# The sample sequences' depthwise convolution as products over windows and sums along the taps

## Chip, cores and metric

One core of a Trainium2 chip runs one launch of the kernel. The metric is the device time in microseconds of that launch, as the median of the runs; lower is better. The profiler's record of one execution gives the durations used below.

## The reference, cut to what matters

The reference runs one layer of a decoder trunk for two groups of tokens that share all weights: a prompt of 1024 tokens, and 8 sample sequences of 8 tokens each. A layer is an FFN, a mixer of two branches (a Conformer convolution and an mLSTM with 4 heads), and a second FFN. The change touches the causal depthwise convolution alone, of width 31 over 1024 channels:

```python
def _causal_dwconv(u, buf, w, b):
    full = jnp.concatenate([buf.astype(u.dtype), u], axis=1)
    y = lax.conv_general_dilated(full, w[:, None, :].astype(u.dtype), window_strides=(1,), padding='VALID',
                                 dimension_numbers=('NWC', 'WIO', 'NWC'), feature_group_count=u.shape[-1])
    return y + b, full[:, -(CONV_WIDTH - 1):]
```

For the prompt `buf` is zero; for each sample sequence it holds the last 30 inputs of its past. Every output is a sum of 31 products, one per tap, plus a bias per channel.

## The kernel before

Everything lies with the features on the 128 partitions and the tokens in the free dimension: 1024 prompt columns and then 64 sample columns (8 sequences of 8), 1088 in all, padded to 1092 so that they split into three PSUM banks of 364. The 1024 features are 8 tiles of 128. All arithmetic is float32.

**The products.** The weights come in units of 128 x 1024. SP loads each (L333), POOL splits it into a high part (L543) and a low part (L545), and PE makes three passes over it (L575: high by high, high by low, low by high). There are two buffers of split weights, so POOL may split a unit only when PE is done with the unit two before it. These two POOL instructions come once per unit, and both read SBUF.

**The mixer** goes head by head (`H` is 4). The first three heads are one loop on each engine, the last is written out. Each head has two sections.

In section A, PE runs 8 units (q, k, v and o of this head), ACT evicts them, and DVE does `taps(h)` (L1365): the depthwise convolution of two feature tiles of this head. Its input lies in `glu` (2 tiles of 30 zeros and 1024 prompt columns) and `glus` (2 tiles, 8 sequences, 30 columns of past and 8 of their own). `taps` copies the two tiles' weights to `dw_cur` (L1370, L1372) and then goes over the 31 taps (L1373). At each tap it drains DVE (L1376) and issues four instructions: for each of the two tiles one over the 1024 prompt columns and one over the 64 sample columns. Tap 0 is a `tensor_scalar` with the bias (L1388), the other 30 are a `scalar_tensor_tensor` (L1390; the profile shows them at the helper's line, L1072) that adds the product of one shifted slice by one weight to the output in `y`. Before tap 15 `prelude(h)` (L1350) prepares the head's gate columns and signals `head_ready`.

In section B, PE runs 8 units (4 in the last head) and threads the pieces of the mLSTM in between, each a chain over PE, ACT and DVE with small tiles (`ktok`, `vaug`, `vws`, `dw`, `tin`, `hn_p`, `hn_s`, `hs_p`, `hs_s`). Its first DVE instruction is the copy to `ap_h` (L1465), which stands behind `taps` in DVE's order. The first piece's transposes to `bank_x` (PE, L748) wait for it. SP waits for `taps_done` (L433) before it loads the next head's past into `glus`.

The order of the work on each engine is the order of the code. Semaphores order the engines against each other, and `drain` orders DVE against itself.

Of the kernel before, what the change touches and what calls it, by code (L numbers as in the profile page):

```python
# [24 lines left out]

ACT = mybir.ActivationFunctionType
F32 = mybir.dt.float32
F32R = mybir.dt.float32r
I32 = mybir.dt.int32

P = 128
D = 1024
KT = D // P
NP = 1024
NB, TB = 8, 8
NT = NP + NB * TB
# [8 lines left out]
CW = 31  # L45
# [5 lines left out]
C1 = HD + 1  # L51
# [76 lines left out]
def trunk(nc, t_in, t_out):  # L128
    with ExitStack() as ctx:

        at = [(nc.sbuf_base + 63) // 64 * 64]

        def region(nbytes):
            start = at[0]
            at[0] += (nbytes + 31) // 32 * 32
            assert at[0] <= nc.sbuf_usable_end, (at[0], nc.sbuf_usable_end)
            return start

        def place(name, shape, dt, offset):
            return nc.alloc_sbuf_tensor_at(name, shape, dt, offset=offset)  # L140

        def own(name, shape, dt=F32):
            return place(name, shape, dt, region(int(np.prod(shape[1:])) * 4))
# [7 lines left out]
        r_x = region(KT * TILE)  # L151
        x = place("x", [P, KT, W], F32, r_x)
        qkvo = place("qkvo", [P, 8, W], F32, r_x)
        a_hi = place("a_hi", [P, KT, W], F32R, r_x)
        a_tmp = place("a_tmp", [P, KT, W], F32, r_x)
        r_y = region(KT * TILE)
        y = place("y", [P, KT, W], F32, r_y)
        a_lo = place("a_lo", [P, KT, W], F32R, r_y)
        work = place("work", [P, KT, W], F32, r_y)
        sg, prod, ss, rstd = (work[:, i] for i in (0, 1, 2, 3))  # L160
# [7 lines left out]
        glu = own("glu", [P, 2, PAST + NP])  # L168
        glus = own("glus", [P, 2, NB, PAST + TB])
        st = own("st", [P, 3, 2, C1])  # L170
        c_cur = own("c_cur", [P, 2, C1])
        ktok = own("ktok", [P, HD])
        vaug = own("vaug", [P, C1])
        vws = own("vws", [P, C1])
        dw = own("dw", [P, P])
        tin = own("tin", [P, C1])
        hn_of = {kind: own(f"hn_{kind}", [P, C1]) for kind in "ps"}
        hs_of = {kind: own(f"hs_{kind}", [P, HD]) for kind in "ps"}
        g_row = own("g_row", [4, NT])
        g_cur = own("g_cur", [4, NT])  # L180
        if at[0] < r_z + KT * TILE:
# [10 lines left out]
        dw_cur = place("dw_cur", [P, 2, CW], F32, r_tmp)  # L192
        b_ada = own("b_ada", [P, NMOD * KT])
        b_in = own("b_in", [P, H, 16])
        vecs = own("vecs", [P, 8, KT])
# [26 lines left out]
        NORM1, NORM2, NORM3, NORMF, B_DW, LN_G, LN_B, MH = range(8)  # L222
# [55 lines left out]
        def bank3(s):  # L278

            return slots[:, s, :, 0:GW]  # L280

        def tile3(ap):
            return ap.rearrange("p (g n) -> p g n", g=3)
# [5 lines left out]
        def sample3(ap64):  # L289
            return ap64.rearrange("p (b t) -> p b t", b=NB)  # L290
# [33 lines left out]
        def _(sp):  # L324
# [75 lines left out]
            def head(h, n_units):  # L400
# [8 lines left out]
                for n in range(n_units):  # L409
# [10 lines left out]
                    if n_units == 4 and n == 3:  # L420
                        for k in range(2, 6):
                            sp.dma_start(qkvo[:, k - 2, :], b_keep[k // 2, :, k % 2, :]).then_inc(b_back[k], 16)
                    load_unit()
                    s, _, freed = jobs.take_unit()
                    t = n // 2 if n_units == 8 and n < 4 else n % 2
                    if n_units == 4 and n == 0:
# [36 lines left out]
            for t in range(2):  # L463
                load_unit()
                load_unit()
                jobs.take_unit()
                s, _, freed = jobs.take_unit()
                sp.wait_ge(slot_free[s], freed)
                sp.wait_ge(glus_in, 32)
                conv_stores(0, t)  # L470
# [370 lines left out]
        def _(act):  # L841
# [6 lines left out]
            def squares(p):  # L848

                for k in range(KT):  # L850
# [6 lines left out]
                    if sqs.n >= 2:  # L857
                        act.wait_ge(sq_added, sqs(-1))
                    act.activation(sq[k % 2][:, 0:NT], x[:, k, 0:NT], ACT.Square).then_inc(sq_done, 1)
                    sqs.add()  # L860

            def root(dst):

                s, done, _ = jobs.take_part()
                act.wait_ge(part_done, done)
                act.activation(tile3(dst), bank3(s), ACT.Sqrt, bias=eps[:, 0:1]).then_inc(slot_free[s], 1)

            def norm(p):
# [3 lines left out]
                for k in range(KT):  # L872
                    act.wait_ge(t_ready, p * KT + k + 1)
                    act.activation(u_hi[:, k, 0:NP], tn[k % 2][:, 0:NP], ACT.Identity, bias=sh[:, k, 0:1])
                    act.activation(u_hi[:, k, NP:NT], tn[k % 2][:, NP:NT], ACT.Copy).then_inc(hi_ready, 1)

            def ffn():
                def gate():
                    s, done, _ = jobs.take_unit()
                    act.wait_ge(unit_done, done)  # L880
                    act.activation(tile3(sg), bank3(s), ACT.Silu).then_inc(slot_free[s], 1)

                def high(j, up):
                    act.wait_ge(slot_free[up[0]], up[2])
                    act.activation(hid_hi[:, j, :], prod, ACT.Copy).then_inc(hid_hi_done, 1)  # L885

# [179 lines left out]
        def _(dve):  # L1066
# [4 lines left out]
            def stt(out, in0, scalar, in1, op0, op1):  # L1071
                return dve.scalar_tensor_tensor(out=out, in0=in0, scalar=scalar, in1=in1, op0=op0, op1=op1)  # L1072
# [259 lines left out]
            for n in range(4):  # L1332
# [4 lines left out]
                src = bank[0:L].rearrange("p (c q e) -> p c q e", c=4, q=4)[:, :, :, 0:4]  # L1337
# [12 lines left out]
            def prelude(h):  # L1350

                of_head = (lambda t, n: t[:, :, h:16:4]) if isinstance(h, int) else (
                    lambda t, n: t.rearrange("p c (q h) -> p c q h", q=4)[:, :, :, bass.ds(h, 1)].rearrange("p c q h -> p c (q h)"))
                sel = ident[0:4, h:h + 1] if isinstance(h, int) else ident[0:4, bass.ds(h, 1)]
                dve.drain()
                dve.wait_ge(c_out, 16 * heads(1))
                dve.wait_ge(b_out, 16 * heads(1))
                dve.tensor_copy(col_h[:], of_head(col[:], NC))
                dve.tensor_copy(cols_h[:], of_head(cols[:], NB))
                dve.tensor_scalar(g_cur[:], g_row[:], sel, -1.0, ALU.mult, ALU.mult)  # L1360
                dve.tensor_scalar(apm[:], apv[:], sel, None, ALU.mult)
                dve.memset(c_cur[:], 0.0).then_inc(head_ready, 1)
                heads.add()

            def taps(h):  # L1365

                tiles = [2 * h, 2 * h + 1]
                pick = lambda t: (y[:, tiles[t], :] if isinstance(h, int) else y[:, bass.ds(tiles[t], 1), :].rearrange("p a n -> p (a n)"))
                if isinstance(h, int):
                    dve.tensor_copy(dw_cur[:], w_dw[:, 2 * h:2 * h + 2, :])  # L1370
                else:
                    dve.tensor_copy(dw_cur[:], w_dw[:, bass.ds(2 * h, 2), :])  # L1372
                for j in range(CW):  # L1373
                    if j == CW // 2:
                        prelude(h)
                    dve.drain()  # L1376
                    if j == 0:
                        dve.wait_ge(glus_in, 32 * heads(1))
                        for t in range(2):
                            dve.wait_ge(conv_out[t], 16 * convs[t]())  # L1380
                    for t in range(2):
                        yt = pick(t)
                        w = dw_cur[:, t, j:j + 1]
                        for out, src in ((yt[:, 0:NP], glu[:, t, j:j + NP]),
                                         (sample3(yt[:, NP:NT]), glus[:, t, :, j:j + TB])):
                            if j == 0:
                                b = vecs[:, B_DW, 2 * h + t:2 * h + t + 1] if isinstance(h, int) else vecs[:, B_DW, bass.ds(2 * h + t, 1)]
                                last = dve.tensor_scalar(out, src, w, b, ALU.mult, ALU.add)  # L1388
                            else:
                                last = stt(out, src, w, out, ALU.mult, ALU.add)  # L1390
                last.then_inc(taps_done, 1)

            def section_a(h):
                taps(h)
                for _ in range(8):
                    jobs.take_unit()
# [96 lines left out]
            for k in range(1, KT):  # L1493
                last = dve.tensor_tensor(ysum, y[:, 0, :] if k == 1 else ysum, y[:, k, :], ALU.add)
# [173 lines left out]
```

## Time and profile before

| quantity | value |
|---|---|
| median of 3 runs | 3418.11 us |
| lowest and highest run | 3416.35 and 3418.35 us |
| span of the profiled execution | 3417.0 us |
| PE busy | 3167.0 us (93%) |
| DVE busy | 1597.9 us (47%) |
| POOL busy | 1020.0 us (30%) |
| ACT busy | 465.6 us (14%) |

The page gives the profiled execution's span, from its first to its last instruction; it gives no separate time for that execution, so the 1.1 us between span and median is taken as what lies around the span. The busy share of an engine is an average over stages with different limits. What section A is worth is read from its own stretch, and from who waits for whom at its end.

### The profile page before, as it was taken

How to read it: one execution, taken by the hardware profiler on the slowest of the kernel's cores; microseconds unless marked ns; L12 is line 12 of the kernel's file. 1: busy time of each engine (PE TensorE's matmuls, PEld its weight loads, DVE VectorE, ACT ScalarE, POOL GpSimd, SP SyncE). 2: the span in 40 equal slices, each digit the busy share in tenths (PEclk: the TensorE clock that was granted, in tenths of full speed). 3: DMA queues.
4: the chain of work that ended last, by engine and by line, in shares of the span. 5: the costliest groups of instructions: out<-in, count | busy, mean ns of one | idle time of the engine just before them, and what ended most of it. 6: DMA issues, size and time to landing. Idle time of an engine off the chain costs nothing.

```text
span 3417.0 us, 47244 instructions
## 1 busy us (share of the span) xinstructions
PE 3167.0 (93%) x18860; PEld 3029.7 (89%) x18860; DVE 1597.9 (47%) x2811; ACT 465.6 (14%) x746; POOL 1020.0 (30%) x449
## 2 busy tenths in 40 slices
PE   8999999999968889879888997989998999999995
PEld 8999999999958778878787895789887999999995
DVE  5122233222276943973694397476344233232335
ACT  2000000000031122012112211322012000000001
POOL 1233333333312311321231142034332333333331
PEclk9999999999989999999999998999998999999997
DMA  6312121212121112212211221222210111111111
GB/s 221 106 62 74 61 74 61 74 61 68 49 75 41 44 42 68 70 34 60 74 50 42 68 70 51 60 103 93 108 50 25 44 44 44 47 43 43 43 43 59
DMA packets 83136, 217.63 MB, mean 64 GB/s; under 512 B 28352, under 2 KB 28480, under 8 KB 82496
## 3 DMA queue, kind: packets, MB, share of 16 engines
q1 hardware_dynamic: 83000, 215.86, 19.7%
q8 instruction: 88, 1.44, 0.2%
q14 instruction: 40, 0.33, 0.0%
q10 hardware_dynamic: 8, 0.00, 0.0%
HBM read 184.03 MB, written 31.81 MB: 63 GB/s over the span
## 4 chain that ended last, share of the span: by engine, by line
PE 73%; DVE 16%; issue 5%; DVEq 3%; POOL 1%; DMA 1%; ACT 1%; SPq 0%; ACTq 0%; POOLq 0%
PE slots L575 61%; DVE y L1072 12%; PE bank_x L637 3%; PE bank_x L758 2%; DVEq L1376 2%; PE bank_x L750 1%; PE bank_x L765 1%; PE bank_y L762 1%; PE bank_y L767 1%; DVE work L1100 1%; PE bank_y L637 1%; DMA w_raw<-w_units_dram 1%; PE bank_y L740 1%; PE bank_x L775 0%; PE bank_x L748 0%
## 5 line engine op out<-in xcount | busy, mean ns | idle before, releaser
L543 POOL TENSOR_TENSOR w_hi<-w_raw,one 128x1024 fp32r<-128x1024 f32 x220 | 437.9, 1990 | 2317.9 <-PE slots L575 2247.3
L575 PE MATMUL slots<-u_hi,w_hi 128*128 128x364 f32 (+1 forms) x4032 | 930.3, 339 | 53.0 <-DVE u_lo L1133 20.2
L575 PE MATMUL slots<-u_hi,w_lo 128*128 128x364 f32 (+1 forms) x4032 | 899.5, 332 | 0.0
L575 PE MATMUL slots<-u_lo,w_hi 128*128 128x364 f32 (+1 forms) x4032 | 898.4, 331 | 0.0
L575 PEld LDWEIGHTS slots<-u_hi,w_hi 128*128 128x128 f32 x4032 | 699.4, 191 | 81.4 <-issue 65.4
L575 PEld LDWEIGHTS slots<-u_hi,w_lo 128*128 128x128 f32 x4032 | 705.3, 190 | 9.2 <-issue 8.7
L575 PEld LDWEIGHTS slots<-u_lo,w_hi 128*128 128x128 f32 x4032 | 708.2, 191 | 0.0
L545 POOL TENSOR_TENSOR w_lo<-w_raw,w_hi 128x1024 fp32r<-128x1024 f32 x220 | 581.3, 2642 | 17.2
L1163 DVE TENSOR_TENSOR work<-work,slots 128x1092 f32<-128x1092 f32 x44 | 56.9, 1292 | 913.5 <-PE slots L575 913.5
L1072 DVE SCALAR_TENSOR_TENSOR y<-glu,dw_cur,y 128x1024 f32 (+1 forms) x240 | 344.7, 1436 | 9.1
L1072 DVE SCALAR_TENSOR_TENSOR x<-slots,m_g,x 128x728 f32<-128x728 f32 x368 | 257.8, 742 | 0.0
L575 PE MATMUL slots<-hid_hi,w_hi 128*128 128x364 f32 (+1 forms) x1056 | 237.4, 333 | 11.1 <-DVE hid_lo L1168 9.6
L575 PE MATMUL slots<-hid_lo,w_hi 128*128 128x364 f32 (+1 forms) x1056 | 233.8, 330 | 0.0
L575 PE MATMUL slots<-hid_hi,w_lo 128*128 128x364 f32 (+1 forms) x1056 | 232.3, 328 | 0.0
L575 PEld LDWEIGHTS slots<-hid_hi,w_hi 128*128 128x128 f32 x1056 | 183.6, 190 | 12.1 <-DVE hid_lo L1168 10.0
L885 ACT ACTIVATE hid_hi<-work 128x1092 fp32r<-128x1092 f32 x44 | 49.2, 1118 | 1030.5 <-PE slots L575 733.7
L575 PEld LDWEIGHTS slots<-hid_lo,w_hi 128*128 128x128 f32 x1056 | 183.5, 189 | 0.0
L575 PEld LDWEIGHTS slots<-hid_hi,w_lo 128*128 128x128 f32 x1056 | 183.3, 189 | 0.0
L1146 DVE TENSOR_TENSOR xs_tmp<-slots,m_g 128x64 f32<-128x64 f32 x184 | 41.4, 225 | 289.1 <-PE slots L575 288.1
L1072 DVE SCALAR_TENSOR_TENSOR y<-glus,dw_cur,y 128x64 f32 (+1 forms) x240 | 149.3, 622 | 0.0
L637 PEld LDWEIGHTS bank_x<-cs,ada 128*128 128x128 f32 x896 | 119.4, 212 | 5.3 <-issue 5.3
L637 PE MATMUL bank_x<-cs,ada 128*128 128x9 f32 x896 | 116.2, 267 | 5.3 <-DMA ada<-ada_units_dram 5.3
(219 smaller groups left out, 2187.4 us busy)
## 6 DMA issues: line engine op xcount, KB each, us to landing
w_raw<-w_units_dram SPq DMA_DIRECT2D x220, 512.0 KB, 3.6
ada<-ada_units_dram SPq DMA_DIRECT2D x72, 512.0 KB, 4.2
st<-state_dram SPq DMA_DIRECT2D x32, 257.0 KB, 3.7
C_s_out<-st SPq DMA_DIRECT2D x32, 257.0 KB, 3.6
x_keep<-x SPq DMA_DIRECT2D x1, 4368.0 KB, 12.7
ga_keep<-th SPq DMA_DIRECT2D x8, 546.0 KB, 5.6
gb_keep<-th SPq DMA_DIRECT2D x8, 546.0 KB, 5.6
th<-gb_keep SPq DMA_DIRECT2D x8, 546.0 KB, 4.6
```

The costliest lines, as they stand in the source:

```text
L543: pool.tensor_tensor(w_hi[:, slot, :], w_raw[:, slot, :], one[:].to_broadcast([P, D]), ALU.mult).then_inc(w_hi_done, 1)
L545: pool.tensor_tensor(w_lo[:, slot, :], w_raw[:, slot, :], w_hi[:, slot, :].bitcast(F32), ALU.subtract).then_inc(w_split, 1)
L575: last = pe.matmul(slots[:, s, g, 0:b - a], w_of(w), r[:, k, a:b], start=(k == 0 and q == 0), stop=(k == K - 1 and q == 2))
L637: last = pe.matmul(b[:, 16 * j:16 * j + NV], ada[:, j, k * P:(k + 1) * P], cs[:, k, :], start=(k == 0), stop=(k == KT - 1))
L740: pe.matmul(bank_y[0:L, 0:L], k_of(m, a, L), q_of(m, a, L), start=(m == 0), stop=(m == 1))
L750: last = pe.matmul(bank_x[0:L, n * P:(n + 1) * P], src, ident[:], start=True, stop=True)
L758: last = pe.matmul(bank_x[0:L, 0:C1], q_of(m, a, L), mem[:, m, :], start=(m == 0), stop=(m == 1))
L885: act.activation(hid_hi[:, j, :], prod, ACT.Copy).then_inc(hid_hi_done, 1)
L1072: return dve.scalar_tensor_tensor(out=out, in0=in0, scalar=scalar, in1=in1, op0=op0, op1=op1)
L1146: dve.tensor_tensor(sample3(xs_tmp[:]), sample3(slots[:, s, 2, LP:LP + NB * TB]), per_batch(g[:, 1:NV]), ALU.mult)
L1163: dve.tensor_tensor(tile3(prod), tile3(sg), bank3(s), ALU.mult).then_inc(slot_free[s], 1)
L1376: dve.drain()
```

## The change

The prompt's 31 steps stay, two instructions a tap instead of four. The sample columns leave the loop. After tap 0 and ahead of tap 1 a new function `conv_of_sample` runs. For each of the two tiles and each half of the 8 sequences it makes one `tensor_tensor` product and one `tensor_reduce`:

- the product reads `glus` through an access pattern of overlapping windows (4 sequences, 8 positions, 31 taps), multiplies it by the tile's 31 weights, repeated over sequences and positions, and writes 992 columns to the new tile `win`;
- the sum goes along the 31 taps and writes 32 columns of `y`.

A drain stands before each of these eight instructions, and another before the two `tensor_scalar` that add the bias to 64 columns each.

`win` has no memory of its own: it lies over `ktok`, `vws`, `dw`, `tin` and part of `hn_p`, which section B uses and section A does not. `vaug`, whose last column of ones must stay, is moved ahead of it.

```diff
@@ -24,6 +24,7 @@
 from concourse.alu_op_type import AluOpType as ALU
 
 ACT = mybir.ActivationFunctionType
+AX = mybir.AxisListType
 F32 = mybir.dt.float32
 F32R = mybir.dt.float32r
 I32 = mybir.dt.int32
@@ -169,13 +170,16 @@
         glus = own("glus", [P, 2, NB, PAST + TB])
         st = own("st", [P, 3, 2, C1])
         c_cur = own("c_cur", [P, 2, C1])
+        vaug = own("vaug", [P, C1])
+        r_win = at[0]
         ktok = own("ktok", [P, HD])
-        vaug = own("vaug", [P, C1])
         vws = own("vws", [P, C1])
         dw = own("dw", [P, P])
         tin = own("tin", [P, C1])
         hn_of = {kind: own(f"hn_{kind}", [P, C1]) for kind in "ps"}
         hs_of = {kind: own(f"hs_{kind}", [P, HD]) for kind in "ps"}
+        win = place("win", [P, NB // 2 * TB, CW], F32, r_win)
+        assert at[0] >= r_win + NB // 2 * TB * CW * 4
         g_row = own("g_row", [4, NT])
         g_cur = own("g_cur", [4, NT])
         if at[0] < r_z + KT * TILE:
@@ -1362,6 +1366,25 @@
                 dve.memset(c_cur[:], 0.0).then_inc(head_ready, 1)
                 heads.add()
 
+            def windows(t, b):
+
+                first = glus[:, t, b:b + NB // 2, 0:TB]
+                return bass.AP(first.tensor, first.offset, [*first.ap, [1, CW]])
+
+            def conv_of_sample(pick, bias):
+
+                for t in range(2):
+                    for b in (0, NB // 2):
+                        dve.drain()
+                        dve.tensor_tensor(win[:].rearrange("p (b t) j -> p b t j", b=NB // 2), windows(t, b),
+                                          dw_cur[:, t, :].unsqueeze(1).unsqueeze(1).to_broadcast([P, NB // 2, TB, CW]), ALU.mult)
+                        dve.drain()
+                        dve.tensor_reduce(pick(t)[:, NP + b * TB:NP + (b + NB // 2) * TB], win[:], AX.X, ALU.add)
+                dve.drain()
+                for t in range(2):
+                    out = pick(t)[:, NP:NT]
+                    dve.tensor_scalar(out, out, bias(t), None, ALU.add)
+
             def taps(h):
 
                 tiles = [2 * h, 2 * h + 1]
@@ -1370,7 +1393,10 @@
                     dve.tensor_copy(dw_cur[:], w_dw[:, 2 * h:2 * h + 2, :])
                 else:
                     dve.tensor_copy(dw_cur[:], w_dw[:, bass.ds(2 * h, 2), :])
+                bias = lambda t: (vecs[:, B_DW, 2 * h + t:2 * h + t + 1] if isinstance(h, int) else vecs[:, B_DW, bass.ds(2 * h + t, 1)])
                 for j in range(CW):
+                    if j == 1:
+                        conv_of_sample(pick, bias)
                     if j == CW // 2:
                         prelude(h)
                     dve.drain()
@@ -1379,15 +1405,12 @@
                         for t in range(2):
                             dve.wait_ge(conv_out[t], 16 * convs[t]())
                     for t in range(2):
-                        yt = pick(t)
+                        out, src = pick(t)[:, 0:NP], glu[:, t, j:j + NP]
                         w = dw_cur[:, t, j:j + 1]
-                        for out, src in ((yt[:, 0:NP], glu[:, t, j:j + NP]),
-                                         (sample3(yt[:, NP:NT]), glus[:, t, :, j:j + TB])):
-                            if j == 0:
-                                b = vecs[:, B_DW, 2 * h + t:2 * h + t + 1] if isinstance(h, int) else vecs[:, B_DW, bass.ds(2 * h + t, 1)]
-                                last = dve.tensor_scalar(out, src, w, b, ALU.mult, ALU.add)
-                            else:
-                                last = stt(out, src, w, out, ALU.mult, ALU.add)
+                        if j == 0:
+                            dve.tensor_scalar(out, src, w, bias(t), ALU.mult, ALU.add)
+                        else:
+                            last = stt(out, src, w, out, ALU.mult, ALU.add)
                 last.then_inc(taps_done, 1)
 
             def section_a(h):
```

## Rows read from the trace of the kernel before

**Rows 1.** The page: its first line, and part 4, the chain that ended last, by line.

```profile
span 3417.0 us, 47244 instructions
...
PE slots L575 61%; DVE y L1072 12%; PE bank_x L637 3%; PE bank_x L758 2%; DVEq L1376 2%; PE bank_x L750 1%; PE bank_x L765 1%; PE bank_y L762 1%; PE bank_y L767 1%; DVE work L1100 1%; PE bank_y L637 1%; DMA w_raw<-w_units_dram 1%; PE bank_y L740 1%; PE bank_x L775 0%; PE bank_x L748 0%
```

**Rows 2.** Waits of PE, whole run and second head; columns: us in total, times, longest.

```profile
PE bank_x L748 <- DVE ap_h L1465: 80.9, 4, 25.5
...
PE bank_x L748 <- DVE ap_h L1465: 17.4, 1, 17.4
```

**Rows 3.** Busy time of each engine in one stretch, the second head's taps.

```profile
core 0: us, PE busy (x) PEld busy (x) DVE busy (x) ACT busy (x) POOL busy (x), PEclk, DMA share, GB/s
1380.73:1504.30 123.57, 106.30 (x630) 105.61 (x628) 120.23 (x131) 12.00 (x11) 42.40 (x16) 0.93 0.13 42
```

**Rows 4.** Line 1072 writing y, all heads (ns min/median/max); last row from page part 5.

```profile
L1072 DVE SCALAR_TENSOR_TENSOR y<-glu,dw_cur,y x240: 1272/1283/3412, 1084.2 to 2096.0; 128x1024 f32 x90, 128x1024 f32<-128x1024 f32 x30
L1072 DVE SCALAR_TENSOR_TENSOR y<-glus,dw_cur,y x240: 271/278/2427, 1085.4 to 2097.2; 128x64 f32 x90, 128x64 f32<-128x64 f32 x30
...
L1072 DVE SCALAR_TENSOR_TENSOR y<-glus,dw_cur,y 128x64 f32 (+1 forms) x240 | 149.3, 622 | 0.0
```

**Rows 5.** Timeline of DVE, start of the second head's taps; columns: start us, us.

```profile
1381.42 0.81 DVE L1388 TENSOR_SCALAR y<-glu,dw_cur,vecs 128x1024 f32 x1 [0.49 <-issue]
1382.15 0.31 DVE L1388 TENSOR_SCALAR y<-glus,dw_cur,vecs 128x64 f32 x1
...
1383.49 1.28 DVE L1072 SCALAR_TENSOR_TENSOR y<-glu,dw_cur,y 128x1024 f32 x1
1384.69 0.28 DVE L1072 SCALAR_TENSOR_TENSOR y<-glus,dw_cur,y 128x64 f32 x1
1384.89 1.28 DVE L1072 SCALAR_TENSOR_TENSOR y<-glu,dw_cur,y 128x1024 f32 x1
1386.08 0.28 DVE L1072 SCALAR_TENSOR_TENSOR y<-glus,dw_cur,y 128x64 f32 x1
1386.44 1.28 DVE L1072 SCALAR_TENSOR_TENSOR y<-glu,dw_cur,y 128x1024 f32 x1
```

**Rows 6.** Timeline of DVE and of POOL around one split of weights, second head.

```profile
1394.92 1.92 DVE L1072 SCALAR_TENSOR_TENSOR y<-glus,dw_cur,y 128x64 f32 x1
1396.91 3.40 DVE L1072 SCALAR_TENSOR_TENSOR y<-glu,dw_cur,y 128x1024 f32 x1
...
1394.17 2.59 POOL L543 TENSOR_TENSOR w_hi<-w_raw,one 128x1024 fp32r<-128x1024 f32 x1 [22.69 <-PE slots L575]
1396.84 2.40 POOL L545 TENSOR_TENSOR w_lo<-w_raw,w_hi 128x1024 fp32r<-128x1024 f32 x1
```

**Rows 7.** Nearest DVE instructions: timeline of a drained series, then lines 1100, 1098, 1279.

```profile
2254.69 8.15 DVE L1494 TENSOR_TENSOR a_tmp<-a_tmp,y 128x1092 f32<-128x1092 f32 x6
...
L1100 DVE TENSOR_TENSOR work<-work x28: 1291/1292/3460, 33.9 to 3388.0; 128x1088 f32<-128x1088 f32 x28
...
L1098 DVE COPY work<-work x4: 727/728/2266, 33.1 to 3367.0; 128x1088 f32<-128x1088 f32 x4
...
L1279 DVE TENSOR_TENSOR_SCAN g_row<-rows,mc x8: 471/472/2652, 1035.2 to 1044.3; 4x128 f32<-4x128 f32 x8
L1279 DVE TENSOR_TENSOR_SCAN g_row<-rows,ms x8: 208/208/224, 1045.0 to 1046.0; 4x8 f32<-4x8 f32 x8
```

**Rows 8.** Timeline in the first FFN: a DVE product that reads PSUM, and POOL.

```profile
567.88 1.29 DVE L1163 TENSOR_TENSOR work<-work,slots 128x1092 f32<-128x1092 f32 x1 [21.71 <-PE slots L575]
...
567.99 1.90 POOL L543 TENSOR_TENSOR w_hi<-w_raw,one 128x1024 fp32r<-128x1024 f32 x1 [9.41 <-PE slots L575]
```

**Rows 9.** Timeline of DVE and of POOL, start of the first head's taps.

```profile
1082.12 0.81 DVE L1388 TENSOR_SCALAR y<-glu,dw_cur,vecs 128x1024 f32 x1 [4.76 <-DMA conv_s_out<-glus]
...
1086.58 2.03 POOL L543 TENSOR_TENSOR w_hi<-w_raw,one 128x1024 fp32r<-128x1024 f32 x1 [11.50 <-PE slots L575]
1088.68 2.39 POOL L545 TENSOR_TENSOR w_lo<-w_raw,w_hi 128x1024 fp32r<-128x1024 f32 x1
```

## The prediction

> **What bounds the kernel now.** I read the page first. The span is 3417.0 us, and the chain that ended last is PE's for 61%, but 12% of it is DVE's line 1072 writing `y`, and 2% more is DVE's queue at L1376, the drain of the tap loop [rows 1]. So the taps are on the path for part of the run. The waits of PE say where: its longest wait is for the copy to `ap_h`, the first DVE instruction behind the taps, four times and 80.9 us in all; in the second head it is 17.4 us [rows 2]. The busy times of the second head's taps agree: in 123.57 us DVE is busy for 120.23, PE for 106.30 [rows 3]. In section A, DVE is the bound of every head, and PE idles for over 17 us at its end. So what `taps` gains or loses, up to 17.4 us a head, goes one to one into the span. What it gains would be lost again only behind PE's own end, which lies far beyond the effects below.
>
> **Why the listed busy time misleads.** The 64-column steps show a median of 278 ns and a maximum of 2427; the 1024-column ones 1283 and 3412 [rows 4]. The page's mean of 622 ns for a 64-column step [rows 4] would make 60 x 0.62 = 37 us a head. I go by start to start instead. In an undisturbed tap the starts are 1383.49, 1384.69, 1384.89, 1386.08 and 1386.44 [rows 5]: the first sample step takes 0.20 us of the time, the second 0.36 (with the drain). A whole tap is 2.95 us.
>
> The long ones come from POOL. When it splits a unit, a sample step takes 1.92 us and the next prompt step 3.40; they end within 0.1 us of the ends of POOL's two instructions, 1396.76 and 1399.24 plus the step itself [rows 6]. DVE loses (1.92 - 0.28) + (3.40 - 1.28) = 3.76 us per split, whichever instruction is hit. POOL has 16 instructions in this stretch [rows 3], so eight splits, one per unit. The account closes: 0.69 (copy and issue) + 2.07 (tap 0) + 30 x 2.95 + 8 x 3.76 = 121.3, which leaves 2.2 us of the 123.6 for the prelude. A removed sample step that stood in a split does not take the stall with it: the next prompt step stands there instead. The splits' times are PE's, and all eight still fall within the taps.
>
> **Removed, per head.** The 30 pairs of `scalar_tensor_tensor`. The next prompt step then starts 1.20 us behind the first, as a step behind a step does now, and the second one is followed by the drain at once. A drained series of DVE instructions shows what that costs: 6 products of 1.30 us take 8.15, so (8.15 - 1.30) / 5 = 1.37 from start to start, a gap of 0.07 [rows 7]. A tap becomes 1.20 + 1.28 + 0.07 = 2.55 us, which saves 0.40; 30 taps save **12.0**. Tap 0 goes from 1383.49 - 1381.42 = 2.07 [rows 5] to 0.73 + 0.81 + 0.07 = 1.61, which saves **0.46**.
>
> **Added, per head.** Four products of 992 columns with both inputs in SBUF. The nearest row is the product of 1088 columns, 1.291 us undisturbed [rows 7]; less 96 columns at (1283 - 278) / 960 = 1.05 ns [rows 4] it is 1.19. Four sums of 992 columns: the trace has no reduction along columns. From below the bound is the copy, 0.728 us for 1088 columns [rows 7], so 0.65. From above it is the scan, the one instruction here that carries a sum: (472 - 208) / 120 = 2.2 ns a column [rows 7], which makes 992 columns 2.37 us. I take 1.19, as for a product, to which it is nearer than to the scan: it reads each column once and hands on one sum per 31. With a gap of 0.07 after each, 4 x (1.19 + 1.19 + 0.14) = **10.1**. The two bias adds of 64 columns are 2 x 0.31 [rows 5] + 0.07 = **0.7**. Together 10.8.
>
> The Trainium skill (VectorE: DVE Perf Modes, the perf-mode tier table) has `tensor_reduce` at one element a cycle in every case; by its 0.96 GHz and the (N + 151) / 0.96 that it gives for a product, an estimate for the sum is 1.19 us, and the total would be as forecast.
>
> **Net** 12.46 - 10.8 = 1.7 us a head, 6.7 us in four.
>
> **The first head gains more.** Its taps start at 1082.12, so the new block runs from 1083.73, and POOL wants the port at 1086.58 [rows 9]. A DVE product of which one input is in PSUM is not held up by POOL: it takes its usual 1.29 us although POOL starts 0.11 us later, and POOL takes its usual 1.90 [rows 8]. A sum also has one SBUF input and runs at one column a cycle in my forecast, so I let it run beside POOL. Walking through: the second product ends at 1087.4 and POOL's first instruction runs to 1089.3 beside the second sum; the third product waits 0.6 us; POOL's second runs to 1092.9 beside the third sum; the fourth product waits 1.1. That is 1.6 lost in place of 3.8, a gain of **2.1**. In the second head (the others are alike) the block begins at 1381.42 + 1.61 = 1383.0, its last sum ends at 1393.1, and POOL begins at 1394.17 [rows 6]: nothing there.
>
> The Trainium skill (SBUF — State Buffer, Who interferes with whom) says the same: two SBUF inputs contend with a reading POOL, and `tensor_reduce` never does. [rows 6] and [rows 8] agree for products.
>
> **Edits at nothing.** Where `win` and `vaug` lie costs no instruction. The signal to SP moves with the end of the taps; its load of `glus` is needed a whole section later. The extra drains find DVE empty. Register work for the new dynamic addresses hides behind the instructions running; uncovered it would be a few tenths a head.
>
> **Sum.** 6.7 + 2.1 = 8.8 us off the profiled span: 3408.2, and with the 1.1 us around it **3409.3 us** (-0.26%). A measurement here can tell about 0.2%, 6.8 us, from no change, so the edge of faster lies at 3411.3, where the sum would take 1.32 us instead of 1.19.
>
> **Rivals.**
>
> 1. *Small prices eat it; no change to be seen.* Sixteen products and sixteen sums stand in the path, so 0.13 us more on one kind costs 2 us. If POOL holds up the sums as well, the first head's gain goes: 3411.4. One mechanism would be the windows themselves: runs of 31 words that start on odd words half the time. Against it, prompt steps start on odd columns at every other tap, and their minimum and median are 1272 and 1283 ns [rows 4]; for it, no row has short odd runs. At one lost column per run, 32 x 1.04 ns x 16 = 0.5 us: 3409.8. With the first head's gain gone and the sums at 1.5 us it is 3416. Chance of this case 0.32.
>  The Trainium skill (Vector Engine (DVE) Microarchitecture Reference, Measured stream behaviour on trn2) gives 1.30 ns a column in place of 1.05 for word pairs starting on an odd word; if the products took that, the total would be 3413.2 by an estimate from its figures. The prompt steps' rows speak against it for long runs; none here shows short ones.
>
> 2. *The sum goes at the scan's rate; slower.* Place: the four `tensor_reduce` of each head, each drained before and after, with nothing beside them on the path. At 2.37 us each, 16 x 1.18 = 18.9 us more than forecast: 3428.2. It decides from 1.19 + 8.8 / 16 = 1.74 us a sum on (no gain left), and shows as slower from 2.17 on. For it: the scan also carries a running value from column to column. Against it: the scans work on only four partitions and are another instruction; nothing else on DVE at full size is that slow but the reciprocal. Chance 0.09.
>
> 3. *The stalls go with the sample steps.* If the time that the sample steps spend blocked went with them, a head would save 37 - 10.8 = 26 us, PE would become the bound, and the 80.9 us of its waits would go: 3337. [rows 6] speaks against it: the prompt step is blocked as well as the sample step. Chance 0.02.
>
> **How the numbers follow.** The forecast case has 0.57, rival 1 0.32, rival 2 0.09, rival 3 0.02. Faster is the forecast with rival 3, less a little for its upper edge, 0.57; same is rival 1 with that little, 0.34; slower 0.09. The range leaves out rivals 2 and 3 and the copy-rate end of the sum (16 x 0.54 = 8.6 us further down, 3400.7), and takes in most of what lies between: 3403 to 3417.
>
> **What would show it.** In the changed profile: prompt steps in a tap at starts 1.20 and 1.35 apart; 16 products and 16 sums near 1.19 us; PE's four waits for `ap_h` down by 1.7 us each, by 3.8 in the first head; POOL's first split of the first head beside a sum; section B of unchanged length. A sum of over 1.3 us, a tap that stays above 2.7 us, or dynamic addresses that leave gaps of issue between the new instructions would prove the forecast wrong.

## The result, and the profile after

| | kernel before | changed kernel |
|---|---|---|
| median of 20 runs | 3418.73 us | 3410.73 us |
| lowest and highest | 3416.35 and 3423.96 us | 3405.28 and 3419.52 us |
| profiled execution, span | 3417.0 us | 3411.4 us |
| DVE busy | 1597.9 us | 1582.5 us |
| PE's waits for `ap_h` | 80.9 us | 71.6 us |

The ratio is 0.9973, with a 95% interval of 0.9967 to 0.9980: 8.0 us less by the medians, where 8.8 less (3409.3 us) was forecast. The changed kernel's runs scatter more widely than those of the kernel before. In its profiled execution the first head's taps start at 1081.5 us, 4.4 us later than in the one of before, and nothing ahead of them was changed. So a span is a poor measure of this change, and I go by the stretches that it touches.

First the page of the changed kernel, its first line and the second of part 4, to be read against [rows 1]:

```profile
span 3411.4 us, 47078 instructions
...
PE slots L579 61%; DVE y L1076 6%; DVEq L1402 6%; PE bank_x L641 3%; PE bank_x L762 2%; PE bank_x L754 1%; PE bank_x L769 1%; PE bank_y L766 1%; PE bank_y L771 1%; DVE work L1104 1%; PE bank_y L641 1%; DVE win L1379 1%; PE bank_y L744 1%; DVE y L1382 1%; DMA w_raw<-w_units_dram 1%
```

DVE's prompt steps and the drain of the tap loop, now L1402, hold 12% of the chain, where the same two groups held 14%. The product (L1379) and the sum (L1382) have joined it with 1% each. The waits of PE say the same, against [rows 2]:

```profile
PE bank_x L752 <- DVE ap_h L1488: 71.6, 4, 21.2
```

The wait is 9.3 us shorter in all and far from gone: DVE is still the bound of section A in every head. What the instructions cost now, from the views of line 1076 and of the tile `win` (ns min/median/max), against [rows 4] and [rows 7]:

```profile
L1076 DVE SCALAR_TENSOR_TENSOR y<-glu,dw_cur,y x240: 1271/1284/3422, 1099.7 to 2088.9; 128x1024 f32 x90, 128x1024 f32<-128x1024 f32 x30
L1379 DVE TENSOR_TENSOR win<-glus,dw_cur x16: 1192/1193/1887, 1087.9 to 1979.7; 128x992 f32<-128x992 f32 x16
L1382 DVE TENSOR_REDUCE y<-win x16: 1185/1186/1189, 1089.2 to 1981.0; 128x992 f32 x12, 128x32 f32<-128x992 f32 x4
```

The undisturbed prompt step is what it was. The product takes 1.193 us where 1.19 was forecast, and the sum, for which the trace of before had no row, takes 1.186 us against 1.19. The sum's 16 durations lie within 4 ns of each other, though POOL works beside some of them. The product's longest is 1.887 us.

The mean of the 240 prompt steps rose from 1436 to 1720 ns on the page, though none was added or changed; that is 68 us more in all. The 149.3 us of the sample steps are gone from the page, and 68 us of them stand in the prompt steps now: it is time for which DVE waits for POOL, listed under the instruction that happens to stand there. (The busy time of the prompt steps rose only by 58.5 us, from 344.7 to 403.2, since the page counts the overlap of two neighbouring steps once.)

The timeline of DVE and then of POOL at the start of the first head's taps, against [rows 9]:

```profile
1086.26 1.53 DVE L1411 TENSOR_SCALAR y<-glu,dw_cur,vecs 128x1024 f32 x2 [4.55 <-DMA conv_s_out<-glus]
1087.87 1.19 DVE L1379 TENSOR_TENSOR win<-glus,dw_cur 128x992 f32<-128x992 f32 x1
1089.23 1.19 DVE L1382 TENSOR_REDUCE y<-win 128x992 f32 x1 [0.17 <-issue]
1090.49 1.19 DVE L1379 TENSOR_TENSOR win<-glus,dw_cur 128x992 f32<-128x992 f32 x1
1091.85 1.19 DVE L1382 TENSOR_REDUCE y<-win 128x992 f32 x1 [0.16 <-issue]
1093.11 1.38 DVE L1379 TENSOR_TENSOR win<-glus,dw_cur 128x992 f32<-128x992 f32 x1
1094.65 1.19 DVE L1382 TENSOR_REDUCE y<-win 128x992 f32 x1 [0.17 <-issue]
1095.91 1.89 DVE L1379 TENSOR_TENSOR win<-glus,dw_cur 128x992 f32<-128x992 f32 x1
...
1090.91 2.52 POOL L547 TENSOR_TENSOR w_hi<-w_raw,one 128x1024 fp32r<-128x1024 f32 x1 [11.48 <-PE slots L579]
1093.52 3.23 POOL L549 TENSOR_TENSOR w_lo<-w_raw,w_hi 128x1024 fp32r<-128x1024 f32 x1
```

The events come in the order of the forecast's walk. POOL wants to start at 1090.91 and waits for the second product to end at 1091.7. It then works beside the second sum, which is not lengthened. The third product waits 0.19 us for it, and the fourth waits 0.70 for POOL's second instruction. The split costs DVE 0.9 us, where 1.6 was forecast. The second profiled execution (e8) has the same two waits, 0.19 and 0.69 us.

The length of section A, from the start of the copy to `dw_cur` to the start of the copy to `ap_h`, in us (both profiled executions of the changed kernel; the second is run e8 below):

| head | before | changed | changed again | forecast saving | measured saving |
|---|---|---|---|---|---|
| 1 | 127.55 | 123.21 | 122.28 | 3.8 | 4.3, 5.3 |
| 2 | 123.50 | 121.72 | 121.52 | 1.7 | 1.8, 2.0 |
| 3 | 123.32 | 121.50 | 121.60 | 1.7 | 1.8, 1.7 |
| 4 | 122.75 | 120.13 | 120.16 | 1.7 | 2.6, 2.6 |
| sum | 497.12 | 486.56 | 485.56 | 8.8 | 10.6, 11.6 |

The spaces between the heads stay as they were within 1.3 us, in both directions (176.0, 174.5 and 172.9 before; 174.8, 175.4 and 172.0 after). From the last head's copy to `ap_h` to the end it is 1319.4 us before and 1321.1 in both executions of the changed kernel; over all kernels of this study that stretch varies from 1316.1 to 1322.2 us.

One thing is new in the taps themselves. In each looped head of the changed kernel DVE pauses once, late in the taps, before an ordinary prompt step; the second head:

```profile
1490.87 10.15 DVE L1076 SCALAR_TENSOR_TENSOR y<-glu,dw_cur,y 128x1024 f32 x8 [0.45 <-issue]
```

The pause is 0.43 to 0.46 us in both executions and in e3. The kernel before, the written-out head and the runs e1, e2 and e4 to e7 do not have it. What makes it is not known.

### The profile page after: what moved, and what is told of

Its sections match the earlier page's. It is cut to its first block, busy times and chain, and to the rows that moved or that the text cites. A ratio compares the mean times of both kernels' runs of the same rounds, so it can differ in the third digit from the quotient of the medians.

```text
span 3411.4 us, 47078 instructions
## 1 busy us (share of the span) xinstructions
PE 3171.8 (93%) x18860; PEld 3033.9 (89%) x18860; DVE 1582.5 (46%) x2603; ACT 465.6 (14%) x746; POOL 1025.7 (30%) x449
## 4 chain that ended last, share of the span: by engine, by line
PE 73%; DVE 11%; DVEq 8%; issue 6%; POOL 1%; DMA 1%; ACT 1%; SPq 0%; ACTq 0%; POOLq 0%
PE slots L579 61%; DVE y L1076 6%; DVEq L1402 6%; PE bank_x L641 3%; PE bank_x L762 2%; PE bank_x L754 1%; PE bank_x L769 1%; PE bank_y L766 1%; PE bank_y L771 1%; DVE work L1104 1%; PE bank_y L641 1%; DVE win L1379 1%; PE bank_y L744 1%; DVE y L1382 1%; DMA w_raw<-w_units_dram 1%
## 5 line engine op out<-in xcount | busy, mean ns | idle before, releaser
L549 POOL TENSOR_TENSOR w_lo<-w_raw,w_hi 128x1024 fp32r<-128x1024 f32 x220 | 589.1, 2678 | 17.3
L1076 DVE SCALAR_TENSOR_TENSOR y<-glu,dw_cur,y 128x1024 f32 (+1 forms) x240 | 403.2, 1720 | 10.2 <-issue 1.3
L579 PEld LDWEIGHTS slots<-hid_hi,w_hi 128*128 128x128 f32 x1056 | 183.5, 190 | 12.5 <-DVE hid_lo L1172 10.0
L641 PE MATMUL bank_x<-cs,ada 128*128 128x9 f32 x896 | 116.2, 267 | 4.9 <-DMA ada<-ada_units_dram 4.9
L885 ACT ACTIVATE work<-slots 128x1092 f32<-128x1092 f32 x44 | 47.6, 1083 | 477.1 <-PE slots L579 477.1
```

The source lines that it names most:

```text
L549: pool.tensor_tensor(w_lo[:, slot, :], w_raw[:, slot, :], w_hi[:, slot, :].bitcast(F32), ALU.subtract).then_inc(w_split, 1)
L579: last = pe.matmul(slots[:, s, g, 0:b - a], w_of(w), r[:, k, a:b], start=(k == 0 and q == 0), stop=(k == K - 1 and q == 2))
L641: last = pe.matmul(b[:, 16 * j:16 * j + NV], ada[:, j, k * P:(k + 1) * P], cs[:, k, :], start=(k == 0), stop=(k == KT - 1))
```

## The experiments

The theory: DVE's order of instructions sets the end of section A. A small step costs what it adds from start to start; a stall behind POOL belongs to the time of the split and not to the step that stands there; a sum along columns runs beside POOL and a product of two SBUF tensors does not. The rivals: the stalls go with the steps, or the place of the block has nothing to do with the gain.

### e1: the sample steps left out, nothing added

```diff
-                            else:
+                            elif out.shape == yt[:, 0:NP].shape:
                                 last = stt(out, src, w, out, ALU.mult, ALU.add)
```

> The kernel before without the 60 sample steps of taps 1 to 30 in each head (the sample columns of y keep tap 0 alone, so those outputs are those of a convolution of width 1). My account: a tap falls from 2.95 to 2.55 us, section A (from dw_cur to ap_h) from 123.5 to 111.5 us in the later heads, the splits still cost 3.76 us each, total 12.0 x 4 = 48 us below the kernel before, about 3371 us; PE's four waits for ap_h fall from 80.9 to about 33 us. Rival: the stalls go with the removed steps (37 us a head): PE becomes the bound, its waits for ap_h vanish, total near 3340 us. Second rival: nothing is gained since each 64-column step fits into a gap that the drain leaves anyway: total stays within 10 us of 3418.

Measured: 3371.25 us, 0.9856 of the kernel before (0.9840 to 0.9872), 47.7 us less by the medians. Section A of the later heads is 110.4, 110.7 and 109.5 us. The waits of PE:

```profile
PE bank_x L748 <- DVE ap_h L1465: 29.4, 4, 13.0
```

The forecast's account gave 3371; the rival with the stalls gave 3340 and wanted this wait to vanish. So 60 sample steps of listed 622 ns, 37 us a head, were worth 12 us a head by the medians. Section A itself became shorter by 12.5, 13.1, 12.7 and 13.2 us, 51.5 in all, where the account had 48; the median does not show these 3.5 us. It also gives the price of the block: the changed kernel is nearly the one of e1 plus the block, and stands 39 us above it, 10 us a head.

### e2: each sum twice

```diff
+                        dve.drain()
+                        dve.tensor_reduce(pick(t)[:, NP + b * TB:NP + (b + NB // 2) * TB], win[:], AX.X, ALU.add)
```

> The changed kernel with each of its 16 sums done twice, a drain between. My account: 16 x (1.19 + 0.07) = 20 us more than the changed kernel, a little over that in the three looped heads (0.1 us of address work each), less whatever a doubled sum takes in beside POOL: 3427 to 3432 us. Rival: the sums are partly free because DVE waits for POOL's splits anyway: under 10 us more, below 3421 us.

Measured: 3420.95 us, 10.2 above the changed kernel's 3410.73: half of what I expected, and close to the rival's bounds (under 10 more, below 3421). Section A is 126.1, 123.4, 123.8 and 122.9 us, 1.7 to 2.9 us longer a head and not 5. DVE and then POOL at the end of the second head's block:

```profile
1391.92 1.19 DVE L1382 TENSOR_REDUCE y<-win 128x992 f32 x1 [0.17 <-issue]
1393.17 1.19 DVE L1384 TENSOR_REDUCE y<-win 128x992 f32 x1
1394.44 2.15 DVE L1379 TENSOR_TENSOR win<-glus,dw_cur 128x992 f32<-128x992 f32 x1
1396.75 1.19 DVE L1382 TENSOR_REDUCE y<-win 128x992 f32 x1 [0.16 <-issue]
1398.02 1.19 DVE L1384 TENSOR_REDUCE y<-win 128x992 f32 x1
...
1393.65 1.89 POOL L547 TENSOR_TENSOR w_hi<-w_raw,one 128x1024 fp32r<-128x1024 f32 x1 [22.52 <-PE slots L579]
1395.62 3.23 POOL L549 TENSOR_TENSOR w_lo<-w_raw,w_hi 128x1024 fp32r<-128x1024 f32 x1
```

Four sums at 1.26 add 5.0 us and push the end of the block across POOL's split at 1393.65. Three sums then run beside POOL at their usual length and only one product waits, for 0.96 us, where such a split costs 3.6 in the taps (two prompt steps of 2.92 and 3.26 us instead of 1.28). 5.0 - 2.6 is 2.4 a head, and 2.4 is the mean of the four lengths' growth; in the second head alone it is 1.7. From start to start a sum takes 1.25 us here, so it has its full price on the path. What I missed was that a longer block gets a split to lie across, so that the change of length and the change of place come together. In effect the rival was right for this run: a sum that lies beside POOL takes the place of a wait, and so is in part free. The next run changes the place alone.

### e3: the block ahead of tap 4

```diff
-                    if j == 1:
+                    if j == 4:
                         conv_of_sample(pick, bias)
```

> The changed kernel with the sample block ahead of tap 4 in place of tap 1, nothing else. By the trace the block then lies across a split of POOL in all four heads, not in the first alone. My account (a sum runs beside POOL, a product does not): a split costs 1.6 us in place of 3.8 in each of the three later heads, 6 to 7 us less than the changed kernel, near 3404 us, the section A of these heads at 119.5 instead of 121.7 us. Rival (POOL holds up sums as well, and the first head's extra gain had another cause): no change against the changed kernel, 3410.7 us, and the sums beside POOL are listed longer than 1.19 us.

Measured: 3402.10 us, 0.9951 of the kernel before (0.9935 to 0.9968), 8.6 below the changed kernel. The same instructions, none fewer. Section A of the later heads is 118.6, 118.6 and 118.4 us, and 123.2 in the first, which had its split already. These four lengths are 7.9 us less than in the changed kernel, and carry the reading better than the medians do: e8 below has the changed kernel at 3407.28 us, which leaves 5.2. The second head's timeline, DVE and then POOL:

```profile
1378.12 7.59 DVE L1076 SCALAR_TENSOR_TENSOR y<-glu,dw_cur,y 128x1024 f32 x6
...
1391.05 1.36 DVE L1379 TENSOR_TENSOR win<-glus,dw_cur 128x992 f32<-128x992 f32 x1
1392.58 1.19 DVE L1382 TENSOR_REDUCE y<-win 128x992 f32 x1 [0.17 <-issue]
1393.84 1.89 DVE L1379 TENSOR_TENSOR win<-glus,dw_cur 128x992 f32<-128x992 f32 x1
1395.89 1.19 DVE L1382 TENSOR_REDUCE y<-win 128x992 f32 x1 [0.17 <-issue]
...
1388.64 2.72 POOL L547 TENSOR_TENSOR w_hi<-w_raw,one 128x1024 fp32r<-128x1024 f32 x1 [22.23 <-PE slots L579]
1391.44 3.23 POOL L549 TENSOR_TENSOR w_lo<-w_raw,w_hi 128x1024 fp32r<-128x1024 f32 x1
```

The sums keep 1.19 us beside POOL, and the two products wait 0.17 and 0.70, so the split costs 0.9 us and not 3.6. The theory's 3404 holds and the rival's 3410.7 does not. The first line also gives the undisturbed tap: six prompt steps in 7.59 us, (7.59 + 0.07) / 3 = 2.55 us a tap, as forecast.

### e4: one product and one sum a tile

```diff
-        win = place("win", [P, NB // 2 * TB, CW], F32, r_win)
+        win = place("win", [P, NB * TB, CW], F32, r_win)
...
-                    for b in (0, NB // 2):
...
+                    dve.tensor_reduce(pick(t)[:, NP:NT], win[:], AX.X, ALU.add)
```

> The changed kernel with one product and one sum of 1984 columns per tile in place of two of 992. My account (fixed part of 0.16 us per instruction, 0.07 us of drain behind it, 0.1 us of address work before a sum in the looped heads): four instructions fewer per head, 4 x 0.23 + 0.2 = 1.1 us a head, 4.5 us in all, near 3406 us; each instruction at 2.22 us. In the first head the longer instructions may take more or less of the split, within 1 us. Rival (a price per row of 31, or a window pattern that costs more when it runs over all eight sequences): no gain, 3411 us or more.

Measured: 3406.81 us, 0.9958 (0.9941 to 0.9975) of the kernel before, 3.9 below the changed kernel, where 4.5 was expected. By the medians alone this is not clear of noise (the interval overlaps that of the changed kernel); the four lengths of section A (123.0, 119.8, 120.0 and 119.3 us) are 4.6 us less in sum. The product takes 2.226 us at the median and the sum 2.220, so 992 further columns cost 1.03 us in either, and the fixed part is 0.16. No price of a row of 31 shows. The second and third head gain 1.9 and 1.5 us, more than the 1.1 of the account: the pause of 0.45 us that the changed kernel has there is absent here.

### e5: e3 and e4 together

The diff is that of e4 with that of e3.

> The changed kernel with one product and one sum of 1984 columns per tile, and the block ahead of tap 4: both edits of the two runs before together. If they are independent, their gains add (4 us for the fewer instructions, 8 us for the place): near 3398 us. If what the fewer instructions gained was itself a matter of where the longer sum lies against POOL's split (its section A was 1.9 us shorter in the second head, where the fixed parts explain 1.1), the gains do not add and it stays near 3402 us.

Measured: 3398.48 us, 0.9930 (0.9914 to 0.9947). Section A is 121.3, 116.5, 116.3 and 116.7 us. By the medians the two gains add, to 12.3 us below the changed kernel. Section A gains more than the two together, 15.6 us against 7.9 and 4.6: in the second head the split costs a single product 0.25 us (2.47 instead of 2.22), where it cost 0.9 in e3.

### e6: ScalarE makes the products

```diff
+            def products(h, t):
+                if t == 0:
+                    act.wait_ge(dw_ready, dws.add())
+                else:
+                    act.wait_ge(win_summed, sums.add())
+                w3 = win[:].rearrange("p (b t) j -> p b t j", b=NB)
+                for j in range(CW):
+                    out, src, w = w3[:, :, :, j], glus[:, t, :, j:j + TB], dw_cur[:, t, j:j + 1]
...
+                        last = act.activation(out, src, ACT.Copy, scale=w)
+                last.then_inc(win_ready, 1)
...
-                    if j == 1:
-                        conv_of_sample(pick, bias)
+                    if j in (SUM_AT, 2 * SUM_AT):
+                        sum_of_sample(pick, j // SUM_AT - 1)
```

> ScalarE makes the products, tap by tap (31 activations of 64 columns per tile, the bias in tap 0's), in its idle time of section A; DVE keeps only one sum of 1984 columns per tile, ahead of taps 5 and 10; three new semaphores order this. My account (DVE's own order is the bound of section A, and two products of 2.2 us, four drains and the bias adds leave it): section A near 113 us in the later heads instead of 121.7, 32 to 38 us below the changed kernel, 3373 to 3379 us; PE's waits for ap_h near 35 us in all. Rival: ScalarE's 62 small instructions take so long (over 0.4 us each with their strided writes) that DVE waits for win or PE for its evictions: then new waits of DVE on win or of PE on slots appear and the total stays above 3390 us.

Measured: 3379.99 us, 0.9883 (0.9866 to 0.9899), section A 113.5, 113.8 and 114.0 us in the later heads. That is 31 us below the changed kernel, a little short of the 32 to 38. The rival's mechanism is absent. The tile `win` in that trace:

```profile
L978 ACT ACTIVATE win<-glus,dw_cur x240: 393/414/442, 1084.4 to 1968.3; 128x64 f32<-128x64 f32 x120
L976 ACT ACTIVATE win<-glus,vecs,dw_cur x8: 496/509/512, 1084.1 to 1960.9; 128x64 f32<-128x64 f32 x8
L1397 DVE TENSOR_REDUCE y<-win x8: 2204/2208/2218, 1097.9 to 1979.9; 128x1984 f32 x6, 128x64 f32<-128x1984 f32 x2
```

ScalarE's steps are listed at 0.41 us, as slow as the rival wanted, but DVE does not wait for `win` anywhere, nor PE for an eviction. PE's waits for `ap_h` are 40.9 us. What is missing lies in the second sum: it starts at 1404.2 us in the second head, and POOL's splits there are 1396.2 to 1402.0 and from 1408.0.

### e7: the second sum moved onto the split

```diff
-SUM_AT = 5
+SUM_AT = (5, 8)
```

> The kernel with ScalarE's products, the second sum ahead of tap 8 in place of tap 10, nothing else. In that kernel's trace (second head) the second sum starts at 1404.2, between two splits (POOL 1396.2 to 1402.0 and from 1408.0); ahead of tap 8 it should start within 1 us of the split at 1396.2. My account: the sum takes 1.5 to 2.2 us of the split beside it, in all four heads, so 6 to 8 us less than the same kernel with tap 10, near 3373 us, section A 111.5 to 112 us. Rival: the place of a sum does not matter (the gain of the late block came from elsewhere): 3380 us again.

Measured: 3370.08 us, 0.9857 of the kernel before (0.9842 to 0.9872), 9.9 us below e6. Section A is 116.2, 111.4, 111.6 and 111.1 us, 1.4 to 2.9 us less than in e6, 8.6 in sum. DVE and then POOL, second head:

```profile
1380.34 2.21 DVE L1397 TENSOR_REDUCE y<-win 128x1984 f32 x1
1382.65 9.74 DVE L1099 SCALAR_TENSOR_TENSOR y<-glu,dw_cur,y 128x1024 f32 x6
1392.31 2.21 DVE L1397 TENSOR_REDUCE y<-win 128x1984 f32 x1
...
1380.95 1.89 POOL L549 TENSOR_TENSOR w_hi<-w_raw,one 128x1024 fp32r<-128x1024 f32 x1 [22.22 <-PE slots L581]
...
1392.97 1.89 POOL L549 TENSOR_TENSOR w_hi<-w_raw,one 128x1024 fp32r<-128x1024 f32 x1 [6.78 <-PE slots L581]
```

Each sum here begins some 0.6 us ahead of POOL and takes 1.6 us of the split beside it. This is the fastest version of the study, and it reaches the time of e1, in which the sample columns were hardly computed at all (3371.25 us).

### e8: the changed kernel again

> The changed kernel once more, beside the same runs of the kernel before. If what moved the total is section A alone, its four lengths repeat within 0.5 us of 123.2, 121.7, 121.5 and 120.1, and what differs between two profiled executions of it lies elsewhere; the ratio stays at 0.997. Rival (the lengths of section A vary with the phase of POOL's splits by microseconds from run to run, and the first profile was a lucky one): lengths nearer to 122.5, a ratio near 0.999.

Measured: 3407.28 us, 0.9964 (0.9952 to 0.9977). Three of the four lengths repeat within 0.2 us; the first is 0.9 us shorter, outside the 0.5 that I had allowed. The wait for the DMA (4.48 us against 4.55) and the split in the block (0.19 and 0.69 us against 0.19 and 0.70) are nearly the same in both. The difference lies in later splits, which meet DVE's order at another moment. The largest part, 0.6 us, is at the prelude. In the first profiled execution:

```profile
1150.70 2.51 DVE L1364 TENSOR_SCALAR g_cur<-g_row,ident 4x1088 f32<-4x1088 f32 x1
1153.14 2.37 DVE L1365 TENSOR_SCALAR apm<-apv,ident 4x16 f32<-4x16 f32 x1
```

and in e8:

```profile
1146.77 1.85 DVE L1365 TENSOR_SCALAR apm<-apv,ident 4x16 f32<-4x16 f32 x1
...
1149.25 2.90 DVE L1076 SCALAR_TENSOR_TENSOR y<-glu,dw_cur,y 128x1024 f32 x1
```

In the first execution both POOL instructions of a split hold up small steps of the prelude, in e8 one small step and one prompt step. So the rival of this run has a part of the truth, in the first head alone. The taps of this execution start at 1077.2 us, like those of before. So the 4.4 us that the first profile lost ahead of them are not a cost of the change. The gain from section A repeats.

## Why the prediction was right

- **The bound.** DVE's order was the bound of section A and still is. Of the 80.9 us of waits 9.3 went, against 8.8 forecast.
- **The removed steps.** 12.46 us a head were forecast. e1, which removes the 60 steps alone, gained 47.7 us against 48.0 for that part. The reading from start to start was right, and the 622 ns of the page were misleading by a factor of three. That the two totals agree within 0.3 us is luck: section A itself gained 51.5. Rival 3 falls with e1, and with the prompt steps, which took over 68 us of stalls.
- **The added block.** Product and sum were priced at 1.19 us each and measured 1.193 and 1.186. For the sum this was a choice and not a derivation: the rows left 0.65 to 2.37 us open, 27.5 us of the total. The middle value held, and rival 2 falls. Of the first rival, neither the odd starts nor POOL beside the sums shows.
- **The first head.** The walk through the split was right in its order and too dear: 0.9 us lost and not 1.6, in both executions. The prediction read from [rows 6] that a held step ends its full length behind POOL. By those rows it does not: the prompt step ends at 1400.31, 1.07 us behind POOL's 1399.24, and not 1.28. In the block each held product also ends 1.05 us behind POOL's end and not 1.19, and POOL's own held instructions end 0.14 sooner than their usual length would have it. Four such hand-overs make 0.5 us; the 0.1 us ahead of each sum that the next point tells of makes the other 0.2. The saving there was 4.3 and 5.3 us against 3.8. That this is the split and not the head is shown by e3: the same block moved across a split in the other heads took another 7.9 us off section A (8.6 by the medians).
- **The address work.** It was put at nothing behind running instructions, with a few tenths a head if uncovered. It is uncovered: in the looped heads 0.17 us pass before each sum and in the written-out head 0.07, 0.4 us a head. The pause late in the taps takes another 0.4 us a head (0.45 in place of the usual gap of 0.07), in the looped heads alone; the forecast had nothing for it.
- **Two errors that cancel.** The fourth head, which has neither of the two pauses, saved 2.6 us and not 1.7. Its block takes 10.6 us from the first product to the first prompt step (1972.16 to 1982.77), 0.2 less than the 10.8 forecast. The other 0.7 us lie in the taps behind it, where a split that meets two prompt steps costs 3.6 us instead of 3.76 (2.92 and 3.26 us in place of twice 1.28), eight times a head. The looped heads have the same two prompt-step durations at their splits and would have saved 2.6 as well; the 0.8 us of pauses bring them back to 1.8. So that they came out at the forecast 1.7 is luck in part. Why a split is cheaper without sample steps was not tried.
- **The total.** Section A gained 10.6 and 11.6 us in the two profiled executions, where 8.8 was forecast. By the medians the gain is 8.0 and, beside the runs of e8, 12.7. In the first profiled execution the difference lies in stretches that were not touched, the 4.4 us ahead of the taps above all; so a total within 1 us of the forecast is closer than the account itself, which was 1.8 and 2.8 us too low for section A.

## What to carry to other kernels

Price a small instruction by what it adds from start to start, not by its listed mean: where another engine holds this one up, the listed mean holds stalls that stay when the instruction goes. Where two engines exclude each other at known moments, place there the instruction that the other engine does not hold up, here the sum, which has one SBUF input. The place of the same instructions was worth nearly as much (e3, 7.9 us of section A) as the change itself (10.6 and 11.6 us).

## What was not expected of the hardware

- ScalarE's 64-column scaled copies with writes 31 words apart are listed at 0.41 us each, but they overlap: in e6, 12 in a row take 3.11 us, 0.25 from start to start.
- The order in which sums and products meet a split changed the time by microseconds: doubling the four sums of a head (e2) cost 2.6 us a head by the medians and not 5.0, since some of them lay beside POOL.
